# A fused decoder step on one core: the last expert block summed by itself in row groups, the overflow section ahead of it, sample rows in quarters, and the last norm shared by three engines

## What is computed

```python
def _post_block(x, feats, w_o, ln1_g, ln1_b, moe, ln2_g, ln2_b):
    h = _layer_norm(DEEPNORM_ALPHA * x + feats @ w_o, ln1_g, ln1_b)
    return _layer_norm(DEEPNORM_ALPHA * h + _hmoe(h, *moe), ln2_g, ln2_b)
```

## Time and profile before

| | us |
|---|---|
| median of 3 runs | 1736.52 (1733.68 to 1740.8) |
| the profiled execution: its time | 1740.22 |
| its span, first to last instruction | 1738.4 |

### The profile page before, as it was taken

One profiled execution on the slowest core, in us unless ns is written; L12 is line 12 of the kernel. 1 busy time (PEld: TensorE's weight loads), 2 busy tenths in 40 slices (PEclk: granted clock), 3 DMA queues, 4 the chain that ended last, 5 costly groups with the idle time before them and its releaser, 6 DMA issues.

```text
span 1738.4 us, 24705 instructions
## 1 busy us (share of the span) xinstructions
PE 1499.7 (86%) x10694; PEld 890.0 (51%) x10694; DVE 589.3 (34%) x1268; ACT 271.0 (16%) x619; POOL 73.4 (4%) x88
## 2 busy tenths in 40 slices
PE   7999999999699999998688698976989688787784
PEld 6888788888577577733232233322433333333231
DVE  2845558668363111182321021210212102120126
ACT  0023210120353100021101112110111011111111
POOL 1220011012010000000000000000000000000000
PEclk9999999999797899998887799887999779888887
DMA  9975477777899897329999999999999999999992
GB/s 345 355 275 184 165 264 266 244 259 256 312 364 355 315 299 292 145 114 422 426 425 428 426 416 398 427 425 425 383 427 425 428 425 426 426 425 426 426 422 79
DMA packets 155163, 597.36 MB, mean 344 GB/s; under 512 B 9056, under 2 KB 115232, under 8 KB 121760
## 3 DMA queue, kind: packets, MB, share of 16 engines
q1 hardware_dynamic: 137296, 500.78, 72.9%
q0 software_dynamic: 9792, 75.57, 11.1%
q10 hardware_dynamic: 7960, 19.37, 2.9%
HBM read 586.62 MB, written 17.48 MB: 348 GB/s over the span
## 4 chain that ended last, share of the span: by engine, by line
PE 33%; DMA 28%; DVE 3%; ACT 1%; issue 0%; SPq 0%; DVEq 0%
DMA arena<-in_w_up 28%; PE ps L1930 9%; PE ps L1872 7%; PE ps L1903 6%; PE ps L1962 5%; PE ps L1953 4%; PE ps L1910 1%; ACT arena L1496 1%; PE ps L1832 1%; PE ps L1863 0%; DVE arena L1819 0%; DVE arena L1825 0%; DVE arena L1826 0%; DVE arena L1815 0%; PE ps L1861 0%
## 5 line engine op out<-in xcount | busy, mean ns | idle before, releaser
L1930 PE MATMUL ps<-arena 128*32 128x256 f32 x4352 | 317.2, 448 | 164.0 <-DMA arena<-in_w_up 162.4
L657 PE MATMUL ps<-arena 128*128 128x264 f32 x1664 | 382.6, 388 | 12.0 <-DMA arena<-in_w_in 12.0
L657 PEld LDWEIGHTS ps<-arena 128*128 128x128 f32 x1664 | 313.9, 191 | 64.6 <-issue 12.8
L1930 PEld LDWEIGHTS ps<-arena 128*32 128x32 f32 x4352 | 179.7, 128 | 306.1 <-issue 250.9
L1731 DVE TENSOR_TENSOR arena<-arena,ps 64x256 f32<-64x256 f32 x34 | 14.4, 425 | 526.6 <-ACT arena L1500 526.6
L1903 PE MATMUL ps<-arena 128*32 128x512 f32 (+1 forms) x816 | 188.6, 1028 | 0.0
L1953 PE MATMUL ps<-arena 128*32 128x512 f32 x1088 | 157.6, 683 | 0.0
L1872 PE MATMUL ps<-arena 128*128 128x264 f32 x512 | 121.9, 396 | 1.4 <-PEq L2076 1.4
L1513 ACT COPY arena<-ps 32x512 f32<-32x512 f32 x136 | 78.3, 576 | 251.4 <-PE ps L1953 250.2
L1872 PEld LDWEIGHTS ps<-arena 128*128 128x128 f32 x512 | 97.5, 193 | 24.1 <-issue 7.8
L1962 PE MATMUL ps<-arena,keep 128*128 128x512 f32 (+3 forms) x216 | 101.9, 627 | 1.1 <-issue 1.1
(11 more groups left out here) (416 smaller groups left out, 1058.2 us busy)
## 6 DMA issues: line engine op xcount, KB each, us to landing
arena<-in_w_gate SPq DMA_DIRECT2D x60, 2048.0 KB, 29.5
arena<-in_w_up SPq DMA_DIRECT2D x60, 2048.0 KB, 32.5
arena<-in_w_down SPq DMA_DIRECT2D x60, 2048.0 KB, 32.1
arena<-in_w_in SPq DMA_DIRECT2D x52, 1024.0 KB, 9.2
arena<-in_w_o SPq DMA_DIRECT2D x16, 1024.0 KB, 10.9
arena<-in_w_down SPq DMA_DIRECT2D x8, 1024.0 KB, 30.9
arena<-in_w_up SPq DMA_DIRECT2D x8, 1024.0 KB, 28.3
arena<-in_w_gate SPq DMA_DIRECT2D x8, 1024.0 KB, 32.4
```

What stands on the lines that cost most here:

```text
L657: last = pe.matmul(ps[:, n % 2, 0:T], ring[:, slot, k, cols], x[:, k, :], start=(k == 0), stop=(k == KT - 1))
L1930: last = pe.matmul(ps[BS * q:BS * q + BS, 0, 0:CHUNK // 2], xs[:, kk * 4 + i, :], ring[:, s, at:at + CHUNK // 2], start=(k == 0), stop=(k ...
```

## The change

It has five parts.

1. **Sample rows in quarters.** The accumulator of the 8 sample tokens, 8 x 2048, becomes `acc_s`, 128 x 512: column quarter c lies on partitions 32c to 32c + 7. The four sample units of a combine become one, whose four products go to four column groups; n_units falls from 12 to 9.
2. **ln1 by one row.** In place of four broadcast loads of 512 KB, GpSimd's queue loads eight pieces of 2 KB to single partitions. TensorE spreads a quarter of the columns over 128 partitions with a product of ones in each of blocks 0 to 3 (`spread`), and VectorE's `residual` reads it from PSUM, in four quarters. ln2's quarters for the sample rows come in eight loads of 64 KB.
3. **The overflow section** stands ahead of the last block, 33, on every engine, with semaphores of its own (o_*). On TensorE it is preceded by a wait for block 32's outputs; the spare products are gone. Block 33's gather comes behind it, no longer in block 32.
4. **The last block summed by itself.** Block 32's combine stands between the two halves of hidden(33), with 32 rows. Block 33's outputs are copied at once as 128 x 512 (`yq`), row group c holding column quarter c. Eight final products have 32 rows each, in four row groups, with gates repeated in each of them (`repeat_gates`, `sel_q`).
5. **The last norm.** For the first 128 tokens ScalarE scales and shifts halves of 1024 columns, GpSimd multiplies with the gain and adds the bias, and SyncE's queue writes each half. VectorE does the second 128 tokens and the sample rows at 512 columns. The sample rows' mean and variance are joined over the four quarters by products of TensorE with a matrix `same`.

The diff, cut:

```diff
-    spare.sort(key=lambda s: last_use[s])
+    spare = sorted((s for s in range(NSLOT) if last_use[s] < final_first), key=lambda s: last_use[s])
...
-    n_units = 12
+    n_units = 9
+    final = NB - 1
...
             over(0)
-            sp.wait_ge(S["f_st"], 48)
+            for half in (0, 1):
+                sp.wait_ge(S["f_half"], half + 1)
+                cols = slice(half * D // 2, (half + 1) * D // 2)
+                sp.dma_start(o["y_p"][0, 0:P, cols], sums_y[:, 0, cols]).then_inc(S["f_st"], 16)
+            sp.wait_ge(S["f_st"], 16 * 7)
+
+        @block.gpsimd
+        def _(pool):
+            pool.wait_ge(S["d_ln_free"], 1)
+            for j, name in enumerate(("ln1_g", "ln1_b")):
+                for c in range(4):
+                    pool.dma_start(ln_rows[BS * c:BS * c + 1, j, :], a[name][:, c * CHUNK:(c + 1) * CHUNK]).then_inc(S["d_ln"], 16)
+            pool.wait_ge(S["d_ln_free"], 5)
...
+            pool.wait_ge(S["f_ln"], 32)
+            for half in (0, 1):
+                cols = slice(half * D // 2, (half + 1) * D // 2)
+                pool.wait_ge(S["f_z"], half + 1)
+                pool.tensor_tensor(sums_y[:, 0, cols], sums_y[:, 0, cols], ln2[0][:, cols], ALU.mult).then_inc(S["f_zg"], 1)
+                pool.wait_ge(S["f_zg"], half + 1)
+                pool.tensor_tensor(sums_y[:, 0, cols], sums_y[:, 0, cols], ln2[1][:, cols], ALU.add).then_inc(S["f_half"], 1)
...
+                if b == final:
+                    pe.wait_ge(S["d_add"], n_units * (N_GROUP - 1))
+                    pe.wait_ge(S["d_ye"], final)
+                    n_over = extra(pe)
+                    over(0)
+                    gather(BS).then_inc(S["d_gath"], 1)
+                    turn_gates(0, BS)
+                    repeat_gates(BS).then_inc(S["d_turn"], 1)
+                    pe.wait_ge(S["d_xg"], b + 1)
+                    turn().then_inc(S["d_xt"], 1)
...
+                last = hidden(slots[0:8], [landed[0:2], [], landed[2:4], []], release, S["used"],
+                              (lambda: combine(N_GROUP - 1, final, N_GROUP, slice(0, BS))) if b == final else None)
...
+                if b < 4:
+                    spread(b)
-            pe.wait_ge(S["d_add"], n_units * (N_GROUP - 1))
-            spare_products(5)
-            n_over = extra(pe)
...
-            for u in range(n_units):
-                if u == 8:
-                    pe.wait_ge(S["f_add"], 1)
-                unit(u, slice(0, BS * (NB % 4)), u % 8).then_inc(S["f_comb"], 1)
+            pe.wait_ge(S["d_add"], n_units * N_GROUP)
+            pe.wait_ge(S["f_y"], 1)
+            for u in range(8):
+                t, c = u // 4, u % 4
+                t0, n = TOK[t]
+                rows = slice(BS * c, BS * c + BS)
+                pe.matmul(ps[:, FINAL_BANK[u], :], sel_q[rows, t0:t0 + n], yq[rows, :], start=True, stop=True).then_inc(S["f_comb"], 1)
...
```

More of the change, by code:

```diff
@@ L1349, in phase_m @@
     ln2_slot = [PLACE[(n_wo + 12 * NE + k) % NSLOT] for k in (0, 1)]
-    spare = [s for s in range(NSLOT) if s not in ln2_slot]
+    final_first = n_wo + 12 * (NE - 1)
     def chunk_slot(e, j):
@@ L1380, in over_slot @@
         fills = (s in PLACE[0:n_wo]) + 1 + c // len(spare)
-        free = last_use[s] + 1 if c < len(spare) else n_wo + 12 * NE + c - len(spare) + 1
+        free = (S["used"], last_use[s] + 1) if c < len(spare) else (S["o_used"], c - len(spare) + 1)
         return s, 16 * fills, free
@@ new lines, in _ @@
+            final_stats(0)
+            v.wait_ge(S["f_std"], 1)
+            done.link(v.reciprocal(rstd[:, 0:1], rstd[:, 0:1]))
+            v.scalar_tensor_tensor(shift[:, 0:1], agg[:, 0, 0:1], -1.0, rstd[:, 0:1], ALU.mult, ALU.mult).then_inc(S["f_rs"], 1)
+            final_stats(1)
+            v.wait_ge(S["f_comb"], 9)
+            done.link(v.tensor_tensor(acc_s, acc_s, ps[:, 1, :], ALU.add))
+            done.link(v.bn_stats(s_stat, acc_s))
+            v.bn_aggr(s_mv, s_stat).then_inc(S["f_smv"], 1)
@@ L1915, in turn_gates, with repeat_gates, hidden @@
                     last = pe.transpose(ps[0:width, 5, t0:t0 + n], pick_w[0:n, t, at:at + width], ident[0:n, 0:n])
-                last.then_inc(S["d_turn"], 1)
-            def hidden(b, slots, landed, release):
-                pe.wait_ge(S["d_xs"], b + 1)
-                if b:
-                    pe.wait_ge(S["d_hb"], b)
+                return last
+            def repeat_gates(at):
+                for t, (t0, n) in enumerate(TOK):
+                    for c in range(4):
+                        last = pe.matmul(ps[BS * c:BS * c + BS, 6, t0:t0 + n], pick_w[0:n, t, at:at + BS], ident[0:n, 0:n], start=True, stop=True)
+                return last
+            def hidden(slots, landed, release, freed, between=None):
                 for i in range(4):
+                    if i == 2 and between:
+                        between()
                     first = 4 * (i // 2) + i % 2
@@ L1998, in _ @@
-            spare_products(5)
-            n_over = extra(pe)
-            def over(i):
-                with pe.If(n_over > i):
-                    slots = [over_slot(12 * i + j)[0] for j in range(12)]
-                    landed = [(full[s], over_slot(12 * i + j)[1]) for j, s in enumerate(slots)]
-                    pe.wait_ge(S["d_sel"], N_GROUP + i + 2)
-                    gather(NB + i, 64)
-                    pe.wait_ge(S["d_add"], n_units * (N_GROUP - 1 + i))
-                    pe.wait_ge(S["d_turned"], N_GROUP + i)
-                    turn_gates(64, BS)
-                    turn(NB + i)
-                    hidden(NB + i, slots[0:8], [landed[0:4:2], landed[1:4:2], landed[4:8:2], landed[5:8:2]], True)
-                    turn_hidden(NB + i)
-                    down(NB + i, slots[8:12], [landed[8 + f:9 + f] for f in range(4)], True)
-                    combine(N_GROUP - 1 + i, NB + i + 1, N_GROUP + i + 1, slice(64, 96))
-                    pe.wait_ge(S["d_add"], n_units * (N_GROUP + i))
-                    if i + 1 < NOVER:
-                        over(i + 1)
@@ L2019, in _ @@
-            over(0)
-            pe.wait_ge(S["d_ye"], NB)
-            pe.wait_ge(S["d_turned"], N_GROUP)
-            pe.wait_ge(S["d_add"], n_units * (N_GROUP - 1))
-            for u in range(n_units):
-                if u == 8:
-                    pe.wait_ge(S["f_add"], 1)
-                unit(u, slice(0, BS * (NB % 4)), u % 8).then_inc(S["f_comb"], 1)
+                pe.wait_ge(S["d_hs"], b + 1)
+                if b:
+                    pe.wait_ge(S["d_ye"], b)
+                last = down(slots[8:12], [down_landed(position[b], f) for f in range(4)], release, S["used"])
@@ new lines, in _ @@
+            pe.wait_ge(S["f_add"], 1)
+            for c in range(4):
+                rows = slice(BS * c, BS * c + BS)
+                last = pe.matmul(ps[rows, 1, :], sel_q[rows, 2 * P:T_WIDE], yq[rows, :], start=True, stop=True)
+            last.then_inc(S["f_comb"], 1)
+            pe.wait_ge(S["f_smv"], 1)
+            pe.wait_ge(S["f_add"], 2)
+            pe.matmul(ps[:, 2, 0:1], same, s_mv[:, 0:1], start=True, stop=True).then_inc(S["f_mean"], 1)
+            pe.wait_ge(S["f_dev"], 2)
```

322 lines of the change are left out of this document (212 added, 110 removed).

## The result

The changed kernel takes 1746.07 us (median of 8 runs, 1741.11 to 1750.38), the kernel before beside it 1735.47 (8 runs): ratio 1.0054, interval 1.0035 to 1.0073. So it is slower, by some 9 us, where 1732.1 was forecast and the range ended at 1740.5. In a later comparison, with more runs, the ratio was 1.0039 (1.0020 to 1.0058): a loss of 6.8 us, which puts it at about 1743, outside the range too. The profiled execution took 1749.09 us with a span of 1746.7, against 1740.22 and 1738.4.

A forecast was written before the change was run, and what follows sets the result against it. Weight transfers bound the kernel until TensorE's last wait, then on-chip work: stream 8.8 us less, end stretch 4.4 more (81.2 against 76.8), net -4.4 from 1736.52 gives 1732.1 us; range 1724 to 1740.5.

The forecast's parts named there:

- Clock: Around block 33's gather: lower TensorE clock after 9.5 us idle, 1.7 us more for hidden(33), 2.7 for gather.
- Combines: Blocks 8 and 16: fewer combine units shorten the busy stretches that make holes in the weight stream, 5.2 us less.
- Bytes: Weight stream: smaller ln1 loads, net of the added small ones, move 1.56 MB less at 426 GB/s, 3.7 us less.
- A: From block 0's first product to block 32's second half; stream savings forecast at 8.8 us, bounds 3.7 and 8.8.
- Start: Blocks 0 to 3: spreads and GpSimd's small loads delay TensorE; cost taken as 0, bounds 0 and some 8 us.
- rival 2: Near block 1: stream runs dry waiting for GpSimd's rows, a hole of 1.8 or 8.1 us; chance 0.12.
- The branch: Ahead of block 33's gather: the overflow jump, uncovered, takes 7.1 us in all; TensorE idles 9.5 us there.
- Rival 1: Overflow branch before block 33: jump is short with nothing queued ahead, 6.0 us less, 1726.1; chance 0.25.
- The passes: Last norm: VectorE's two passes over the second 128 rows take 4.9 us.
- rival 3: Last norm: GpSimd and VectorE block each other, up to 3 us more, 1735.1; chance 0.13.
- B: From block 32's second half to block 33's last product; forecast to have 15 us moved ahead of down(33).
- C: From block 33's last product to the end; forecast 15 us less after down(33), 25.9 against 41.2.

The follow-up runs named there:

- experiment 5: Changed kernel without GpSimd's eight ln2 quarter transfers; ScalarE copies the quarters from the full rows in the last norm; ratio 1.0030 to the kernel before.
- experiment 2: Changed kernel with each spread of the first norm's rows one block later, those of quarters 2 and 3 both behind block 3; ratio 1.0034 to the kernel before.
- experiment 3: Changed kernel with block 32's sum, between the halves of hidden(33), over 128 rows instead of 32; ratio 0.9998 to the kernel before.
- experiment 1: Changed kernel with TensorE's count load and conditional overflow bodies left out; ratio 0.9999 to the kernel before.
- experiments 6 to 11: Changed kernel with later spread and the kernel before's order at the end, each run building on the one before it; ratios 0.9904 to 0.9856 to the kernel before.
- 6: Changed kernel with later spread, block 33 gathered in block 32, both summed together after the last block, overflow section behind; ratio 0.9904 to the kernel before.
- experiment 8: Restored-order kernel with TensorE's tail written twice, plus GpSimd taking only half of the first tile's norm, VectorE the other; ratio 0.9888 to the kernel before.

## Why the prediction was wrong

A loss came where a gain of 4.4 was forecast. Three steps failed. The stream was to save 8.8 us and saved 5.4, because the new small transfers were priced by their bytes alone and the start at nothing. The clock was to cost 4.4, for the idle time before the gather; the pieces named under Clock took 6.9 more than priced, none of it at the gather, and half of it came from products over 32 rows. VectorE's passes were taken at 4.9, with the meeting with GpSimd left out of the sum; they took 8.2. Point by point, in the prediction's own steps:

- **Combines**: right. 4.9 us of holes went, 5.2 were forecast.
- **Bytes**: mis-sized. The eight 64 KB transfers were priced by their bytes at the full rate, 1.2 us. Into 32 partitions each they held the DMA engines busy at a lower rate (370 GB/s): 3.9 by the windows, and without them A is 2.7 shorter (experiment 5).
- **Start**: taken as 0; rival 2 happened, small. The last row landed at 796.7. The bound of rival 2, 794.6, is 797.7 in this trace, which runs 3.1 later, so the row was in time. But TensorE had idled 5.4 us for it and its clock was down (0.50): the spread took 3.78 for 1.7, and the first slot came free 3.8 after block 1's start for 2.1. The step that failed took both from rows at the full clock. The hole cost 1.9 by its window, and 1.1 in experiment 2. One of the prediction's own signs of being wrong, a DMA share under 0.9 near 800, came true (0.87).
- So A fell by 5.4 instead of 8.8, inside the bounds of 3.7 and 8.8.
- **The branch**: right, 9.77 idle for 9.5 forecast, and removing it took 7.2 of them away. Rival 1 is out.
- **Clock**: wrong in its cause, and 2.5 too small. 4.4 were set aside. Gather took 5.49 at a granted clock of 0.64, no longer than at 1.00, so the 2.7 for it were wrong. In their place block 33's halves took 11.4 for 7.1 and the middle sum 9.9 for 7.7, and 0.4 came at the sum before it, which ran at the full clock: nine units take 8.06, not 7.7. Of these 6.9, 3.4 are due to the 32 rows of the middle sum (experiment 3), which the prediction did not see: it priced a unit by its columns. And the idle time of 9.5 us, on which it put the surcharge, is not what brings it: with 2.56 us the halves and the sum took 22.1 together, for 21.3 (experiment 1). Why the clock is down at the start of hidden(33) stays open.
- **The passes**: rival 3, given 0.13, came true at 3.3 us (8.2 for 4.9), near its price of 3.
- The rest of the stretch was rebuilt within 0.4 per step; the last transfers took 3.7 for 4.5. 81.2 + 2.5 + 3.3 - 0.8 = 86.2, which is what was measured.
- Ahead of the stretch block 32's second half took 6.59 for 5.33, at a lower clock: 1.3, the luck of the run (5.0 to 6.6 in the 14 traces).

So the forecast of -4.4 was wrong by 3.4 in A, 1.3 at its end, and 5.0 behind it, which makes the +5.2 of the traces but for rounding. The timed loss is 9.4 and 6.8 us, each within 3.3. That the rest of it is in part ahead of block 0, where the code is the same, can't be excluded by so few traces.

**What the prediction did not compare.** It took the end stretch as work that no transfer holds up, in both kernels, and in that it was right. It also saw that 15 us would go ahead of down(33) for 15 behind it; they became 23.7 for 13.1. But it did not ask how close the weights were: B is 40.3 to 40.7 where their landing sets it (experiments 6 to 11), and it was 41.0 before. So B had nothing left to give, and whatever was added to it was paid in full. Added were the idle time with the branch (9.8), which before lay behind block 33 under the spare products; a sum of its own for block 32 (9.9), which before was part of the last sum; the slower halves of hidden(33) (4.5); the copy, turn and scalings behind the gather, for which TensorE now waits (2.8); and the 1.3 of luck. The shorter sum of blocks 28 to 31 gave 4.7 back. In C all this bought 5.6 against before's order (28.1 and 33.7); the other 7.5 of C's gain come from the sample quarters and the shared norm and cost nothing in B. With the same norm in before's order, the traces are 18.5 us shorter (977.0 in experiment 2, 958.5 in 6).

**The range** failed by treating its misses as alternatives. Each took the sum over the others' good case. Here 3.4 in the stream, 2.5 at the clock and 3.3 in the passes came together, with 1.3 of luck and 0.8 the other way: 1732.1 + 9.7 = 1741.8, outside the range, with none of them large.

## What to carry to other kernels

Before moving work about at the end of a stream, find out when its last piece lands: work that is done by then is free, and what is added beyond it is all paid. Here B was full already. Keep a far jump off the path: let the likely case be the one that goes on, and jump when the engine is done. Where several small costs have the same sign and don't exclude one another, add them up in the range.

## What the hardware showed

- A branch of TensorE that goes on takes 0.089 us, one that jumps over the overflow bodies 4.0 to 6.3.
- Products over 32 rows of the array let TensorE's clock fall from the higher level (2.4 GHz) to the lower (1.2 GHz) although it was busy throughout: in six traces of six, within the middle sum (1.00, then 0.50 in the changed kernel). The same number of products over 128 rows, after the same idle time ahead of the block, kept it at 1.00 (one trace). The sum took 9.9 us for 8.1, and 13.2 in the trace in which the clock fell earliest. Over 64 rows, in the last sum, the clock held in six traces and was down for the whole sum in one (experiment 8).
- Eight products over four row groups took 2.0 us, and over one group of 64 rows 7.1: row groups do run beside each other. For VectorE's adds of 0.69 each this was worth little at the higher clock (0.86 a unit), but 64-row units at the lower one (1.7) cost the run of experiment 8 some 4 us.
- Gather at a mean granted clock of 0.64 took 5.49 us, at 1.00 5.43.
- Transfers into 32 partitions with 2 KB each kept the DMA engines at a share of 1.03 and at 370 GB/s instead of 427.
